# Sample attention in tiles of 128 cache positions with 4 KB rows, and conditioning slabs every two and a half chunks

## The chip, the cores and the metric

The kernel runs on one core of one Trainium2 chip. The metric is the device time of one execution, in microseconds; three runs of the kernel before gave 1655.76, 1656.50 and 1656.68 us, median 1656.5 us. Everything is float32.

## The reference

One layer of a hybrid decoder, for a prompt of 256 tokens and for 8 sample sequences of 4 new tokens each (32 rows), with the same weights. D_MODEL is 2048.

```python
mod = silu(c) @ w_ada + b_ada                      # 6 x 2048 columns: shift, scale, gate, twice
h = rmsnorm(x) * (1 + scale1) + shift1
qa, ka, va, qb, kb, vb, r, log_a = project(h)      # one matrix w_in, 2048 x 6160
oa = mix_a(qa, ka, va)                             # 16 heads of 64: attention, three dilations merged
ob, gla_state = mix_b(qb, kb, vb, log_a)           # 4 heads: gated linear attention
x = x + gate1 * merge_out(oa, ob, r)               # w_out, 2048 x 2048
h2 = rmsnorm(x) * (1 + scale2) + shift2
x = x + gate2 * conv_ffn(h2)                       # w_up, convolution, w_down
```

For the samples, mix_a attends from each new token to a cache of 1024 past keys and values per sequence (`cache_k_win`, `cache_v_win`, shape 8 x 1024 x 16 heads x 64) and to the 4 new ones. Of the older 512 cache positions only 4 in 16 are ever seen, so 128 + 512 = 640 cache positions (CK) per sequence are used, that is KT = 5 tiles of 128.

## The kernel before

**Order of the work.** TensorE runs one long sequence and the other engines feed it. It computes the first conditioning columns, then the input projection in 96 chunks (the loop `for j in range(LAST)`), with the rest of the conditioning, the GLA heads and the prompt's attention pairs put between the chunks at fixed chunk numbers; then the sample attention in four groups of two sequences (the stage that the change rewrites); then the output projection, the up-projection and the down-projection. A weight product is three matmuls (L921 to L923) on a high and a low part of each operand; the parts of a weight chunk are made by ScalarE (L1453, L1461, L1470) and VectorE (L1995 and others) from a slab in `ring`.

**Conditioning slabs.** The later conditioning, 48 slabs of 4 x 512 columns of `w_ada` (1 MB each, rows of 2 KB), comes in pairs. `LATE_AT` gives the chunk after which TensorE uses slab r (`late_ada`, L872): 22, 22, 25, 25, ... 91, 91. Slab r goes into ring slot 1 or 3, and there is one pair of slots: ScalarE's queue issues the load of slab r (`late_load`, L1513) only when TensorE has used slab r - 2. After each fourth slab `late_turn` transposes the result. In the same code `in_load` loads the slabs of w_in into slots 0 and 2 from SyncE's queue, and GpSimd's queue moves the GLA states. `head(h, r)` is step r of GLA head h at chunk 28 + 8h + r, `pair(p, r)` is step r of pair p at chunk 63 + 4p + r. A pair computes scores at step 2 (L1113); VectorE and ScalarE make probabilities of them; step 4 transposes these (L1121); step 5 is the product with the values (L1130).

**Sample attention.** A group has 16 key units n: unit (i, j) is all 640 positions of one head pair of one sequence. `key_turns` transposes its five tiles (L1168) into two PSUM banks, of which units with even n are copied to `kcT` by ScalarE (L1643, L1645) and those with odd n by VectorE (L2255, L2257); both also copy 32 new keys behind them (L1644, L2256). `kcT` has 8 buffers, PSUM space is two units. `scores` (L1183) is eight matmuls per j, in two halves of 336 positions, accumulated over j = 0 to 3 in banks 4 and 5. When the last is done, VectorE adds the bias and takes the maximum (`maxima`, L2267, L2270), ScalarE takes the exponential (L1649), VectorE normalizes (L2277), TensorE transposes the probabilities (L1200), ScalarE copies them (L1654 to L1656), TensorE multiplies them with the values (L1213, then the new values, L1220), ScalarE copies the result (L1661) and TensorE transposes it (L1226). TensorE's order in a group g is: units 4 to 7 of g; probabilities and values of g - 1; units 8 to 11; output of g - 1; units 12 to 15; last scores; units 0 to 3 of g + 1. VectorE copies units, then runs maxima(g) before it copies the first units of g + 1.

**Loads of the stage.** SyncE's queue issues them in its program's order. A slab u of keys is one sequence with half of the heads (512 columns, rows of 2 KB): 256 KB for the old positions and 1 MB for the near ones (L606, L607), in ring slot u. The values come likewise in pieces of 256 and 512 KB (L629, L630, L635) into `vals`, which lies over the space of hhi and hlo. The keys of g + 1 are issued as the units of g that use the slot are transposed, the values of g when `values` of g - 1 has passed tile 2 (`v0`) and its end (`v`). The first keys wait for the last two conditioning slabs (`raw_used`, slots 1 and 3) and for the last w_in slabs (slots 0 and 2); the first values wait for TensorE's last chunks. Before the values of the last group SyncE issues two slabs of `w_ada` (`gate_load(0)`, `gate_load(1)`), after them two of w_out (`out_half`) and two more of w_ada.

## Time and profile before

| | |
|---|---|
| median of three runs | 1656.5 us (1655.76 to 1656.68) |
| the profiled execution | 1655.58 us, span 1654.0 us |
| mean granted TensorE clock | 0.994 |
| TensorE (PE) busy | 1612.3 us (97%) |
| VectorE (DVE) busy | 891.0 us (54%) |
| ScalarE (ACT) busy | 719.2 us (43%) |
| DMA, mean over the span | 224 GB/s |
| issue to landing, ring<-in_w_ada from ACT's queue, 58 | median 8.4 us |
| issue to landing, ring<-in_cache_k_win, 1 MB, 16 | median 9.8 us |

PE is the matmuls, PEld the weight loads that overlap them, "q" behind an engine's name its DMA-issuing queue. A busy PE is not PE at its peak: matmul ends are modelled and overlap, so short idle times vanish in the busy share and are read from starts in the timeline instead. "PEclk" is the granted TensorE clock as a share of full speed, 1.00 being 2.4 GHz and 0.50 being 1.2 GHz. A load's time to landing runs from its issue to the arrival of its last part.

### The profile page before, as it was taken

To read this page: it belongs to the slowest core of one execution; us is meant where nothing else is said; L and a number is where in the kernel's file an instruction comes from. 1 tells how busy PE (TensorE), PEld (TensorE's weight loads), DVE (VectorE), ACT (ScalarE), POOL (GpSimd) and SP (SyncE) were. 2 spreads that over 40 slices of the span, in tenths; PEclk is the share of its full clock that TensorE was granted. 3 is DMA by queue.
4 is the path that set the end of the run, shared out by engine and by line. 5 is a ranking of instruction groups with operands and counts; after the bars stand their busy time and mean duration, and the time that the engine had idled before them with its cause. 6 is when DMAs were issued, how large, how long until landed. Compare 5 with 4: busy or idle time off the path is not lost.

```text
span 1654.0 us, 29469 instructions
## 1 busy us (share of the span) xinstructions
PE 1612.3 (97%) x12258; PEld 1445.7 (87%) x12258; DVE 891.0 (54%) x1562; ACT 719.2 (43%) x1026; POOL 75.2 (5%) x132
## 2 busy tenths in 40 slices
PE   8999999999999889999999999999999999999997
PEld 4778888888888544998999999999999999999997
DVE  3555555455665443644754555545555466656563
ACT  3332444445555433534533433334333345555452
POOL 2000000000111000000000000000000000000000
PEclk8999999999999999999999999999999999999999
DMA  9998777778877999675845445454454545545550
GB/s 342 372 379 314 260 248 240 274 266 288 280 251 273 339 380 351 220 241 171 288 148 177 162 155 180 150 182 158 154 181 157 177 132 178 187 159 173 174 171 34
DMA packets 276113, 370.71 MB, mean 224 GB/s; under 512 B 8273, under 2 KB 192947, under 8 KB 275977
## 3 DMA queue, kind: packets, MB, share of 16 engines
q1 hardware_dynamic: 232928, 279.88, 50.6%
q10 hardware_dynamic: 35970, 71.45, 12.1%
q0 software_dynamic: 7088, 17.54, 3.2%
q8 instruction: 97, 1.59, 0.4%
q14 instruction: 30, 0.25, 0.0%
HBM read 358.96 MB, written 9.88 MB: 223 GB/s over the span
## 4 chain that ended last, share of the span: by engine, by line
PE 84%; issue 5%; DVE 4%; DMA 3%; ACT 2%; SPq 1%; POOL 0%; ACTq 0%; DVEq 0%; POOLq 0%
PE ps L921 23%; PE ps L922 22%; PE ps L923 22%; PE ps L872 4%; PE ps L1168 2%; DMA ring<-in_w_in 1%; PE ps L1183 1%; SPq L525 1%; PE ps L1213 1%; DMA vals<-in_w_ada 1%; DMA proj<-in_w_ada 1%; PE ps L879 1%; DVE wlo L1995 1%; ACT whi L1470 0%; PE ps L1097 0%
## 5 line engine op out<-in xcount | busy, mean ns | idle before, releaser
L921 PE MATMUL ps<-hhi,whi 128*128 128x288 f32 x3136 | 934.7, 298 | 1.4 <-DVE hlo L1987 0.7
L922 PE MATMUL ps<-hlo,whi 128*128 128x288 f32 x3136 | 921.9, 294 | 0.0
L923 PE MATMUL ps<-hhi,wlo 128*128 128x288 f32 x3136 | 921.8, 294 | 0.0
L921 PEld LDWEIGHTS ps<-hhi,whi 128*128 128x128 f32 x3136 | 588.3, 188 | 40.0 <-issue 33.4
L922 PEld LDWEIGHTS ps<-hlo,whi 128*128 128x128 f32 x3136 | 588.5, 188 | 0.9
L923 PEld LDWEIGHTS ps<-hhi,wlo 128*128 128x128 f32 x3136 | 588.4, 188 | 0.0
L1856 DVE TENSOR_TENSOR wlo<-ring,whi 128x1024 fp32r<-128x1024 f32 x178 | 212.1, 1222 | 85.8 <-ACT whi L1453 85.4
L1453 ACT ACTIVATE whi<-ring 128x1024 fp32r<-128x1024 f32 x178 | 184.6, 1057 | 156.4 <-PE ps L923 156.4
L1995 DVE TENSOR_TENSOR wlo<-ring,whi 128x1024 fp32r<-128x1024 f32 x96 | 117.3, 1224 | 124.0 <-ACT whi L1470 123.9
L1470 ACT ACTIVATE whi<-ring 128x1024 fp32r<-128x1024 f32 x96 | 100.8, 1052 | 137.6 <-PE ps L923 112.7
L2484 DVE TENSOR_TENSOR wlo<-ring,whi 128x1024 fp32r<-128x1024 f32 (+1 forms) x94 | 105.7, 1131 | 56.0 <-ACT whi L1778 56.0
L1778 ACT ACTIVATE whi<-ring 128x1024 fp32r<-128x1024 f32 (+1 forms) x94 | 91.7, 980 | 73.8 <-PE ps L923 73.7
L2398 DVE TENSOR_TENSOR hlo<-proj,hhi 128x1152 fp32r<-128x1152 f32 (+3 forms) x56 | 60.9, 1100 | 47.5 <-ACT hhi L1725 46.6
L1725 ACT ACTIVATE hhi<-proj 128x1152 fp32r<-128x1152 f32 (+3 forms) x56 | 52.7, 954 | 49.7 <-PE ps L923 49.7
L2419 DVE TENSOR_SCALAR work<-work,small 128x304 f32<-128x304 f32 x44 | 17.3, 436 | 99.5 <-ACT work L1737 99.5
L872 PE MATMUL ps<-ring,c 128*32 128x512 f32 x544 | 68.7, 619 | 1.0 <-DMA ring<-in_w_ada 1.0
L1736 ACT ACTIVATE work<-ps 128x512 f32<-128x512 f32 x22 | 13.2, 599 | 109.3 <-PE ps L923 109.2
L2431 DVE TENSOR_TENSOR proj<-ps,work 128x512 f32<-128x512 f32 x22 | 15.2, 692 | 84.3 <-PE ps L923 84.3
L1168 PEld LDWEIGHTS ps<-con,ring 128*128 128x128 f32 x320 | 35.2, 143 | 24.1 <-issue 12.4
L1461 ACT ACTIVATE whi<-ring 128x1024 fp32r<-128x1024 f32 x32 | 33.2, 1055 | 47.9 <-PE ps L923 29.2
L1168 PE MATMUL ps<-con,ring 128*128 128x128 f32 x320 | 43.8, 283 | 8.5 <-DVE kcT L2257 5.8
L1863 DVE TENSOR_TENSOR wlo<-ring,whi 128x1024 fp32r<-128x1024 f32 x32 | 38.1, 1221 | 16.4 <-ACT whi L1461 16.3
(312 smaller groups left out, 1184.4 us busy)
## 6 DMA issues: line engine op xcount, KB each, us to landing
ring<-in_w_up SPq DMA_DIRECT2D x88, 1024.0 KB, 5.1
ring<-in_w_ada ACTq DMA_DIRECT2D x58, 1024.0 KB, 8.4
ring<-in_w_in SPq DMA_DIRECT2D x48, 1024.0 KB, 9.2
ring<-in_w_down SPq DMA_DIRECT2D x32, 1408.0 KB, 6.7
ring<-in_cache_k_win SPq DMA_DIRECT2D x16, 1024.0 KB, 9.8
vals<-in_cache_v_win SPq DMA_DIRECT2D x32, 512.0 KB, 8.3
ring<-in_w_out SPq DMA_DIRECT2D x16, 1024.0 KB, 6.0
proj<-in_w_ada SPq DMA_DIRECT2D x14, 1024.0 KB, 10.7
```

The source lines that it names most:

```text
L872: last = mm(ps[32 * k:32 * k + 32, bank, :], c32[:, 4 * (s % 4) + k, :], rows[:, k, :], start=(s % 4 == 0), stop=(s % 4 == 3))
L921: mm(out, w_hi, x_hi, start=start, stop=False)
L922: mm(out, w_hi, x_lo, start=False, stop=False)
L923: return mm(out, w_lo, x_hi, start=False, stop=stop)
L1168: last = turn(ps[:, 2 * (n % 2) + t // 4, P * (t % 4):P * (t % 4) + P], slab(u, KT, 512)[:, t, P * m:P * m + P], ident)
L1453: f(whi[:, j % BUFS, 0:n], ring[:, s % SLOTS, n * (j % 2):n * (j % 2) + n], ACT.Copy).then_inc(hi_done, 1)
L1470: f(whi[:, j % BUFS, :].rearrange("p (k c) -> p k c", k=4), in_chunk_of(rows, j), ACT.Copy).then_inc(hi_done, 1)
L1778: f(whi[:, jj % BUFS, 0:n], ring[:, s % SLOTS, CHUNK * kc:CHUNK * kc + n], ACT.Copy).then_inc(hi_done, 1)
L1856: v.tensor_tensor(wlo[:, j % BUFS, 0:n], ring[:, s % SLOTS, n * (j % 2):n * (j % 2) + n], whi[:, j % BUFS, 0:n].bitcast(F32), ALU.subtract ...
L1995: v.tensor_tensor(wlo[:, j % BUFS, :].rearrange("p (k c) -> p k c", k=4), in_chunk_of(rows, j), whi[:, j % BUFS, :].bitcast(F32).rearrange ...
L2398: last = v.tensor_tensor(hlo[:, at:at + m, :], actT[:, k0:k0 + m, :], hhi[:, at:at + m, :].bitcast(F32), ALU.subtract)
L2484: v.tensor_tensor(wlo[:, jj % BUFS, 0:n], ring[:, (2 * kg + h) % SLOTS, CHUNK * kc:CHUNK * kc + n], whi[:, jj % BUFS, 0:n].bitcast(F32), A ...
```

## The change

Keys, values and scores of a group are cut by tiles of 128 cache positions instead of by head halves. A slab `t` of keys or values holds 128 positions of both sequences of the group with all heads: 1 MB in rows of 4 KB (tile 0, the old positions, in two DMAs of 512 KB). A key unit is eight transposes into two PSUM banks, the first bank copied by ScalarE and the second by VectorE, each in one copy of 512 columns; there are 10 units in a group. Scores follow two units behind the transposes and run across the border between groups; the new keys are multiplied straight from `kS` (`new_scores`), not copied. `kcT` shrinks to four buffers. maxima, softmax and normalization of g - 1 are placed between the copies of group g, and two buffers `qd` take turns. SyncE's order of loads and their waits follow the tiles. And `LATE_AT` puts the pairs of conditioning slabs at chunks 22, 24, 27, 29, ... 79.

```diff
-        vals = sb("vals", [P, 4, KT * 512])
-        kcT = sb("kcT", [P, 8, CK + NS])
+        valsf = sb("vals", [P, 2 * KT * 1024])
+        kcT = sb("kcT", [P, 4, 1024])
...
-        qd = projf[:, kv0:kv0 + 512]
+        qd = [projf[:, kv0 + 512 * n:kv0 + 512 * n + 512] for n in range(2)]
...
-        LATE_AT = [22 + r // 2 * 3 for r in range(48)]
+        LATE_AT = [22 + r // 2 * 5 // 2 for r in range(48)]
...
-        def key_tile(n):
-            j, i = n // 4, n % 4
-            return i, j, 2 * (i // 2) + 1 - j // 2, 2 * (i % 2) + j % 2
+        def key_unit(n, e):
+            return [(2 * e + q // 2, n // 4 * 2 + q % 2, n % 4) if n < 8 else (q, KT - 1, 2 * (n - 8) + e) for q in range(4)]
...
-        HALF_KEYS = (CK + NS) // 2
+        KEY_AT = (1, 4, 0, 3, 2)
+        VALUES_AT = (0, 5120, 2048, 7168)
+        ringf = ring[:, :, :].rearrange("p s c -> p (s c)")
+        def key_slab(t):
+            return ringf[:, 2048 * KEY_AT[t]:2048 * KEY_AT[t] + 2048].rearrange("p (b c) -> p b c", b=2)
+        def value_slab(t):
+            if t < KT - 1:
+                return valsf[:, VALUES_AT[t]:VALUES_AT[t] + 2048].rearrange("p (b c) -> p b c", b=2)
+            return valsf.rearrange("p (b c) -> p b c", b=2)[:, :, 4096:5120]
+        def arrived(t, g):
+            return (g + 1) * (32 if t == 0 else 16)
...
-            def key_loads(g, us):
-                for u in us:
-                    sp.wait_ge(*ST.upto(f"k{8 * (1 - u % 2) + 5 + u // 2 * 2}", g - 1))
-                    key_load(g, u)
...
+            def cache_tile(cache, g, t, dst, landed):
+                if t == 0:
+                    for b in range(2):
+                        far = a[cache][0][2 * g + b, 0:PAST // 2].rearrange("(a r) h d -> a r (h d)", r=16)[:, 0:TS]
+                        sp.dma_start(dst[:, b, :], far).then_inc(landed, 16)
+                else:
+                    s_ = PAST // 2 + P * (t - 1)
+                    near = a[cache][0][2 * g:2 * g + 2, s_:s_ + P].rearrange("b p h d -> p b (h d)")
+                    sp.dma_start(dst, near).then_inc(landed, 16)
+            def keys(g, t):
+                cache_tile("cache_k_win", g, t, key_slab(t), keys_in[t])
+            def values(g, t):
+                cache_tile("cache_v_win", g, t, value_slab(t), vals_in[t])
+            sp.wait_ge(raw_used, RAW_OUT - 1)
+            keys(0, 0)
+            sp.wait_ge(raw_used, RAW_OUT)
+            keys(0, 1)
+            sp.wait_ge(lo_done, CH_OUT - 2)
+            keys(0, 2)
+            sp.wait_ge(lo_done, CH_OUT)
+            keys(0, 3)
+            keys(0, 4)
             sp.wait_ge(used, CH_OUT + BUFS - 2)
-            values_first(0, (0, 2))
+            values(0, 0)
+            values(0, 1)
             sp.wait_ge(used, CH_OUT + BUFS)
-            values_first(0, (1, 3))
-            values_last(0)
-            key_loads(1, (1, 3, 0, 2))
-            with sp.Fori(1, NB // 2 - 1) as g:
-                key_loads(g + 1, (1, 3))
-                value_loads(g)
-                key_loads(g + 1, (0, 2))
-            gate_load(0)
-            gate_load(1)
-            value_loads(NB // 2 - 1)
-            sp.wait_ge(*ST.upto("k15", 3))
+            for t in range(2, KT):
+                values(0, t)
+            for g in range(NB // 2):
+                more = g < NB // 2 - 1
+                if more:
+                    sp.wait_ge(*ST[1].upto("k3", g))
+                    keys(g + 1, 0)
+                    keys(g + 1, 1)
+                    sp.wait_ge(*ST[1].upto("k7", g))
+                    keys(g + 1, 2)
+                    keys(g + 1, 3)
+                else:
+                    gate_load(0)
+                    gate_load(1)
+                if g:
+                    sp.wait_ge(*SO.upto("v0", g - 1))
+                    for t in range(3):
+                        values(g, t)
+                    sp.wait_ge(*SO.upto("v", g - 1))
+                    for t in range(3, KT):
+                        values(g, t)
+                if more:
+                    sp.wait_ge(*ST[1].upto("k9", g))
+                    keys(g + 1, 4)
+            sp.wait_ge(*ST[1].upto("k7", 3))
             out_half(0)
+            sp.wait_ge(*ST[1].upto("k9", 3))
             out_half(1)
...
             def key_turns(g, n):
-                i, j, u, m = key_tile(n)
-                if j % 2 == 0 and i % 2 == 0:
-                    pe.wait_ge(far_in[u], g * 16 + 16)
-                    pe.wait_ge(full[u], g * 16 + (SL_SAMP // SLOTS * 16 + 16 - LESS[u]))
-                pe.wait_ge(*SK[n % 2].upto(f"k{(n - 2) % 16}", g if n >= 2 else g - 1))
-                for t in range(KT):
-                    last = turn(ps[:, 2 * (n % 2) + t // 4, P * (t % 4):P * (t % 4) + P],
-                                slab(u, KT, 512)[:, t, P * m:P * m + P], ident)
-                last.then_inc(*ST.step(f"k{n}"))
-            def scores(g, j, half):
-                if j + half == 0:
+                for t in {0: (0, 1), 4: (2, 3), 8: (4,)}.get(n, ()):
+                    pe.wait_ge(keys_in[t], arrived(t, g))
+                for e in range(2):
+                    pe.wait_ge(*SK[e].upto(f"k{(n - 2) % 10}", g if n >= 2 else g - 1))
+                    for q, (i, t, j) in enumerate(key_unit(n, e)):
+                        c = P * head_pair(i, j)
+                        last = turn(ps[:, 2 * (n % 2) + e, P * q:P * q + P], key_slab(t)[:, i // 2, c:c + P], ident)
+                    last.then_inc(*ST[e].step(f"k{n}"))
+            def query(g, i, j):
+                return qd[g % 2][:, 32 * (4 * i + j):32 * (4 * i + j) + 32]
+            def scores(g, n):
+                if n == 0:
                     pe.wait_ge(*SQ.upto("qd", g))
                     pe.wait_ge(*SV.upto("biased", g - 1))
-                if half == 0:
-                    for e in range(2):
-                        pe.wait_ge(*SK[e].upto(f"k{4 * j + 2 + e}", g))
-                cols = slice(HALF_KEYS * half, HALF_KEYS * half + HALF_KEYS)
-                for i in range(4):
-                    q = qd[:, 32 * (4 * i + j):32 * (4 * i + j) + 32]
-                    last = mm(ps[32 * i:32 * i + 32, 4 + half, 0:HALF_KEYS], q, kcT[:, (4 * j + i) % 8, cols],
-                              start=(j == 0), stop=(j == 3))
-                if half:
-                    last.then_inc(*ST.step(f"b{j}"))
-            def key_batch(g, j):
-                for half in range(2):
-                    for n in range(2):
-                        key_turns(g, 4 * j + 2 * half + n)
-                    if j:
-                        scores(g, j - 1, half)
+                for e in range(2):
+                    pe.wait_ge(*SK[e].upto(f"k{n}", g))
+                if n < 8:
+                    for i in range(4):
+                        last = mm(ps[32 * i:32 * i + 32, 4, 256 * (n // 4):256 * (n // 4) + 256], query(g, i, n % 4),
+                                  kcT[:, (2 * g + n) % 4, 256 * i:256 * i + 256], start=(n % 4 == 0), stop=(n % 4 == 3))
+                else:
+                    for j in (2 * (n - 8), 2 * (n - 8) + 1):
+                        for i in range(4):
+                            c = 512 * (j % 2) + P * i
+                            last = mm(ps[32 * i:32 * i + 32, 5, 0:P], query(g, i, j), kcT[:, (2 * g + n) % 4, c:c + P],
+                                      start=(j == 0), stop=(j == 3))
+                last.then_inc(*SB.step(f"s{n}"))
+            def new_scores(g):
+                for j in range(4):
+                    for i in range(4):
+                        mm(ps[32 * i:32 * i + 32, 5, P:P + NS], query(g, i, j), kS[:, head_pair(i, j), :],
+                           start=(j == 0), stop=(j == 3))
...
-                for u in range(4):
-                    pe.wait_ge(vals_in[u], g * 32 + 32)
                 for t in range(KT):
-                    if t == 3:
-                        pe.wait_ge(last_vals_in, g * 64 + 64)
+                    pe.wait_ge(vals_in[t], arrived(t, g))
                     for i in range(4):
-                        rows, b, at = slice(32 * i, 32 * i + 32), i // 2, 512 * t + 256 * (i % 2)
-                        last = mm(ps[rows, 7, :], sT[:, t, rows], vals[:, 2 * b:2 * b + 2, at:at + 256],
-                                  start=(t == 0), stop=False)
+                        rows, at = slice(32 * i, 32 * i + 32), 256 * (i % 2)
+                        v_rows = value_slab(t)[:, i // 2, :].rearrange("p (h c) -> p h c", h=2)[:, :, at:at + 256]
+                        last = mm(ps[rows, 7, :], sT[:, t, rows], v_rows, start=(t == 0), stop=False)
...
-            key_batch(0, 0)
             for g in range(NB // 2):
-                key_batch(g, 1)
-                if g:
-                    probabilities(g - 1)
-                    values(g - 1)
-                key_batch(g, 2)
-                if g:
-                    output(g - 1)
-                key_batch(g, 3)
-                for half in range(2):
-                    scores(g, 3, half)
-                if g < NB // 2 - 1:
-                    key_batch(g + 1, 0)
+                for n in range(0, 10, 2):
+                    key_turns(g, n)
+                    key_turns(g, n + 1)
+                    if n or g:
+                        for m in range(2):
+                            scores(g if n else g - 1, (n - 2) % 10 + m)
+                    if n == 2:
+                        new_scores(g)
+                    if n == 4 and g:
+                        probabilities(g - 1)
+                    if n == 6 and g:
+                        values(g - 1)
+                    if n == 8 and g:
+                        output(g - 1)
+            for m in range(2):
+                scores(NB // 2 - 1, 8 + m)
...
             def key_copy(g, n):
-                i, j = key_tile(n)[0:2]
-                act.wait_ge(*ST.upto(f"k{n}", g))
-                act.wait_ge(*ST.upto(f"b{(j - 2) % 4}", g if j >= 2 else g - 1))
-                f(kcT[:, n % 8, 0:512], ps[:, 0, :], ACT.Copy)
-                f(kcT[:, n % 8, CK:CK + NS], kS[:, head_pair(i, j), :], ACT.Copy)
-                f(kcT[:, n % 8, 512:CK], ps[:, 1, 0:P], ACT.Copy).then_inc(SK[0].sem, 1)
+                act.wait_ge(*ST[0].upto(f"k{n}", g))
+                act.wait_ge(*SB.upto(f"s{(n - 4) % 10}", g if n >= 4 else g - 1))
+                f(kcT[:, (2 * g + n) % 4, 0:512], ps[:, 2 * (n % 2), :], ACT.Copy).then_inc(*SK[0].step(f"k{n}"))
...
-            key_copy(0, 0)
-            key_copy(0, 2)
             for g in range(NB // 2):
-                key_copy(g, 4)
-                key_copy(g, 6)
+                for n in range(4):
+                    key_copy(g, n)
+                if g:
+                    softmax(g - 1)
+                for n in range(4, 6):
+                    key_copy(g, n)
                 if g:
                     probabilities(g - 1)
+                for n in range(6, 8):
+                    key_copy(g, n)
+                if g:
                     output(g - 1)
-                for n in range(8, 16, 2):
+                for n in range(8, 10):
                     key_copy(g, n)
-                if g < NB // 2 - 1:
-                    key_copy(g + 1, 0)
-                softmax(g)
-                if g < NB // 2 - 1:
-                    key_copy(g + 1, 2)
+            softmax(NB // 2 - 1)
...
             def queries(g):
-                dve.wait_ge(*ST.upto("b3", g - 1))
+                if g >= 2:
+                    dve.wait_ge(*SB.upto("s9", g - 2))
...
             def key_copy(g, n):
-                i, j = key_tile(n)[0:2]
-                dve.wait_ge(*ST.upto(f"k{n}", g))
-                dve.wait_ge(*ST.upto(f"b{(j - 2) % 4}", g if j >= 2 else g - 1))
-                v.tensor_copy(kcT[:, n % 8, 0:512], ps[:, 2, :])
-                v.tensor_copy(kcT[:, n % 8, CK:CK + NS], kS[:, head_pair(i, j), :])
-                v.tensor_copy(kcT[:, n % 8, 512:CK], ps[:, 3, 0:P]).then_inc(SK[1].sem, 1)
+                dve.wait_ge(*ST[1].upto(f"k{n}", g))
+                dve.wait_ge(*SB.upto(f"s{(n - 4) % 10}", g if n >= 4 else g - 1))
+                v.tensor_copy(kcT[:, (2 * g + n) % 4, 512:1024], ps[:, 2 * (n % 2) + 1, :]).then_inc(*SK[1].step(f"k{n}"))
...
             queries(0)
-            key_copy(0, 1)
-            key_copy(0, 3)
             for g in range(NB // 2):
-                for n in range(5, 16, 2):
-                    if g and n == 13:
-                        output(g - 1)
+                for n in range(2):
                     key_copy(g, n)
-                maxima(g)
+                if g:
+                    maxima(g - 1)
+                for n in range(2, 4):
+                    key_copy(g, n)
+                if g:
+                    norm_scores(g - 1)
+                for n in range(4, 8):
+                    key_copy(g, n)
                 if g < NB // 2 - 1:
                     queries(g + 1)
-                    key_copy(g + 1, 1)
-                norm_scores(g)
-                if g < NB // 2 - 1:
-                    key_copy(g + 1, 3)
+                for n in range(8, 10):
+                    key_copy(g, n)
+                if g:
+                    output(g - 1)
+            maxima(NB // 2 - 1)
+            norm_scores(NB // 2 - 1)
             output(NB // 2 - 1)
```

## Rows read from the trace of the kernel before

**Rows 1.** Windows: us; PE, PEld, DVE, ACT, POOL busy; PEclk, DMA share, GB/s.
```profile
156.00:546.00 390.00, 384.44 (x2978) 320.27 (x2976) 217.41 (x482) 197.78 (x331) 38.41 (x58) 1.00 0.78 268
...
564.10:590.50 26.40, 22.80 (x207) 12.40 (x203) 11.98 (x46) 10.68 (x31) 0.00 (x0) 1.00 0.89 313
590.50:616.80 26.30, 22.49 (x205) 12.37 (x202) 11.93 (x46) 9.40 (x30) 0.00 (x0) 1.00 1.05 399
616.80:643.00 26.20, 22.89 (x194) 12.76 (x193) 11.93 (x46) 9.40 (x30) 0.00 (x0) 0.93 1.02 373
```
**Rows 2.** Timeline of PE, a group's inside and its border (start, us, what).
```profile
552.60 1.31 PE L1168 MATMUL ps<-con,ring 128*128 128x128 f32 x10
553.84 0.77 PE L1183 MATMUL ps<-kcT,proj 128*32 128x336 f32 x8
554.54 1.31 PE L1168 MATMUL ps<-con,ring 128*128 128x128 f32 x10
...
562.85 1.34 PE L1183 MATMUL ps<-kcT,proj 128*32 128x336 f32 x16 [0.46 <-DVE kcT L2257]
564.11 1.31 PE L1168 MATMUL ps<-con,ring 128*128 128x128 f32 x10
...
568.01 1.64 PE L1168 MATMUL ps<-con,ring 128*128 128x128 f32 x10 [1.33 <-DVE kcT L2257]
...
570.54 0.77 PE L1183 MATMUL ps<-kcT,proj 128*32 128x336 f32 x8
...
575.05 4.50 PE L1213 MATMUL ps<-vals,work 128*32 128x512 f32 x40 [0.99 <-ACT work L1656]
...
580.47 0.33 PE L1168 MATMUL ps<-con,ring 128*128 128x128 f32 x1
```
**Rows 3.** Groups by form, 564 to 616.8 us: the two copies (busy, mean ns).
```profile
L2255 DVE COPY kcT<-ps 128x512 f32<-128x512 f32 x16 | 11.1, 692 | 24.7 <-PE ps L1168 24.7
L1643 ACT ACTIVATE kcT<-ps 128x512 f32<-128x512 f32 x16 | 9.5, 594 | 18.7 <-PE ps L1168 18.6
```
**Rows 4.** DMA view: the first line 547.08 to 548.5 us, the second 639.74 to 639.80.
```profile
vals<-in_cache_v_win SPq DMA_DIRECT2D x1, 512.0 KB, 11.1
...
vals<-in_cache_v_win SPq DMA_DIRECT2D x1, 512.0 KB, 9.7
```
**Rows 5.** Timeline of PE: the stage's last transposes.
```profile
656.14 0.65 PE L1226 MATMUL ps<-con,proj 128*128 128x128 f32 x4
```
**Rows 6.** Windows, columns as in rows 1: a stall and the clock after it.
```profile
617.00:621.00 4.00, 2.15 (x17) 1.71 (x17) 3.87 (x17) 2.60 (x8) 0.00 (x0) 1.00 1.05 407
621.40:624.80 3.40, 3.39 (x19) 1.88 (x17) 1.84 (x6) 0.88 (x3) 0.00 (x0) 0.50 1.05 408
```
**Rows 7.** Timeline: conditioning pairs on PE, and the issue of a second slab.
```profile
372.44 1.92 PE L872 MATMUL ps<-ring,c 128*32 128x512 f32 x16
385.83 1.92 PE L872 MATMUL ps<-ring,c 128*32 128x512 f32 x16
...
446.05 1.92 PE L872 MATMUL ps<-ring,c 128*32 128x512 f32 x16
...
448.04 0.38 ACTq L1513 DMA_DIRECT2D ring<-in_w_ada  x1
```
**Rows 8.** DMA view, second slabs issued at 448.04 and 287.18 us: time to landing.
```profile
ring<-in_w_ada ACTq DMA_DIRECT2D x1, 1024.0 KB, 8.7
...
ring<-in_w_ada ACTq DMA_DIRECT2D x1, 1024.0 KB, 13.9
```
**Rows 9.** Timeline of PE: scores and probability transposes of pairs 4 and 7.
```profile
472.77 0.93 PE L1113 MATMUL ps<-proj 64*128 64x128 f32 x8
...
482.11 0.82 PE L1121 MATMUL ps<-con,proj 128*128 128x128 f32 x6
...
535.62 0.93 PE L1113 MATMUL ps<-proj 64*128 64x128 f32 x8
542.91 0.82 PE L1121 MATMUL ps<-con,proj 128*128 128x128 f32 x6
```

64 lines of the change are left out of this document (13 added, 51 removed).

## The prediction

> **What bounds the kernel now.** The windows by stage come first. In the input projection PE is busy 384.4 of 390 us and the DMA engines have room, at 0.78. In the sample stage that turns round: a group takes 26.4, 26.3 and 26.2 us, PE's busy time leaves over 3 us of each open, and the DMA share is 1.05 and 1.02 in the last two, at 399 and 373 GB/s [rows 1]. So two things set this stage: TensorE's order with its stops, and the loads. The timeline shows the stops, which the busy share hides. Inside a group, ten transposes and a half of scores repeat every 1.94 us [rows 2]. At the border they don't: the last scores begin at 562.85, and six units' transposes, 30 x 0.107 = 3.2 us of work, fill the 6.3 us from 564.11 to 570.4, just before the next scores, waiting for VectorE's copies, which stand behind maxima. Together with the 0.46 us before the last scores that is 3.5 us a group. The probabilities' copy costs another 1 us before 575.05, as nothing is put between.
>
> **The new order on TensorE.** A group has 80 transposes before and after (16 x 5, now 10 x 8) and 8 x 336 = 2688 columns of scores, each four matmuls side by side (now 8 x 256 + 4 x 128 + 4 x 32 = 2688). By the rows a transpose is 0.107 us (a period of 1.94 less 0.70 of scores and 0.17 of changing over, by ten) and 336 columns of scores 0.56 us plus 0.14 of changing over. After: five rounds of 16 x 0.107 + 0.17 + 0.85 + 0.14 = 2.87 us, 14.4 us in all, where eight rounds of 1.94 made 15.5. No row shows matmuls of 32 columns in groups of four; from their columns the 16 of new_scores are 0.2 us, as the same columns cost them before, and at most 0.9 us, one change-over each; I take 0.5, nearer the rate of the 336-column rows. Values and their new rows stay at 5.4 us (575.05 to 580.47 [rows 2]), probabilities 0.6, output 0.45. A group is then 21.4 us on TensorE if nothing waits. The waits: a copy is 0.59 us on ScalarE and 0.69 on VectorE [rows 3], two of each a round of 2.87 us, so the two PSUM pairs are free in time. maxima now stands behind two copies; its 1.9 us of bias and maximum lie beside two units of transposes, 1.7 us, and two scores, 0.85 us. The probabilities' copy has a whole round before values. With these hidden, PE's own chain through four groups would be 20 us shorter than now. If the cover of VectorE is gone, a round waits about 0.7 us, one copy.
>
> **The loads don't follow.** A group needs 5 MB of keys and 5 of values, 10.5 million bytes. In 21.4 us that would be 490 GB/s; the highest figure in my rows is 408 and a whole group reached 399 [rows 1, 6]. So the loads take the place of PE's waits. What must land between the last values of the first group and those of the last is 15 + 15 + 2 slabs of 1 MB (the two gate slabs are issued ahead of the last values), 33.6 million bytes. Before, it ran from 558.2 (547.1 + 11.1) to 649.4 (639.8 + 9.7) [rows 4], 91.2 us, a mean of 368 GB/s, with an idle time of 2 to 3 us before the second key slabs of group 2, since these waited for transposes. After, the first group's values land some 4 us earlier, at 554, because its keys no longer crowd them: with conditioning over at chunk 79, two key slabs are issued at 506, when SyncE is through with the slabs of w_in, instead of 523. And the keys of g + 1 are asked for from unit 3 on, so the queue doesn't run dry. At 399 GB/s, 84 us from 554 ends at 638; at 373 it is 90 us and 644. No row has loads with 4 KB rows; below, I allow them 373, the slowest of the busy groups, above, the 408 of rows 6. I take 393, near the busiest group, and 640.5. Behind the last tile stand one value product, the new values, a copy and the last transposes, 3 us, so the stage ends near 643.5 instead of 656.6 [rows 5]: 13 us less, 9.5 to 16 with the ends of the rate. The Trainium skill (DMA: Bandwidth & Descriptors, section Bandwidth) gives about 358 GB/s as HBM's limit for one core; by that the loads would end at 648 and 5 to 6 us would be gained. The trace disagrees, with 399 GB/s over 26 us [rows 1].
>
> **The clock.** Before, PE stopped for half of a stretch of 4 us, and the granted clock was then 0.50 of full speed, 1.2 GHz, for 3.4 us [rows 6]; that is at most 1.7 us of work lost. After, PE waits about 5 us for the last values, and the same can follow. I charge 1.5 us (0 to 4). The Trainium skill (TensorE: Matmul & The Clock Gate, section HAM oscillation — how this bites in real kernels) says that a wait for DMA takes the clock down, so that the work behind it runs cold; by that a load-bound end is dearer than PE's idle time alone. The rows show one such fall, behind a wait for copies.
>
> **The conditioning slabs.** This is the part that can lose. The work of 48 slabs and 12 late_turns stays, so their moving costs nothing itself; ScalarE's 46 DMA issues move with them, and its queue waits no longer than now, as each waits for a slab that TensorE has just used. But a pair's successor is asked for only when it is used, and the gaps are now alternately two and three chunks. The second slab is issued 2.0 us after the pair's start [rows 7] and takes 8.7 us in a plain case, 13.9 in the worst [rows 8], where states are moved too. It is needed 0.9 us after the next pair's start. So a gap must be 9.8 us in the plain case. The shortest three-chunk gaps are 13.4 us (372.44 to 385.83 [rows 7]); without one bare chunk of 24 matmuls at 0.131, 3.2 us with its change, a gap is 10. From the chunks' own times I get 9.2 (chunk 27 to 29), 9.6 (37), 9.2 (62), 10.3 (52), 10.1 (77) and 10.8 or more for the other seven of the twelve. In the plain case 27, 37 and 62 lose 0.2 to 0.6 each; 37 and 52 lie beside state moves and lose up to 2 and 3 us. Below, nothing is lost; above 6.5 us; I take 2.5, of which 0.5 is no loss, since TensorE waits for VectorE in chunk 54 anyway. Second, in chunks 82 to 91 slabs cover a wait of the pairs. In pair 4 the step from scores to probability transposes took 9.3 us with slabs between; in pair 7, with none, it took 7.3 [rows 9], hardly more than the 6.5 of two bare chunks, so VectorE's chain can be just in time; where it first splits a weight chunk, 1.2 us on the page (L1856), it is that much late. Three pairs lose their cover: 0 to 1.2 us each, and I take 0.5. That makes 3.5 us, 0 to 10.
>
> **Moved and free.** Out_half(0) is asked for earlier, and it lands after the last values as before, some 3 us ahead of its use; gate slabs 2 and 3 land four slabs behind the last values, near 651, and are used behind the first product of the output stage, when before they landed no earlier against the stage's end. SyncE's issues fall from 20 to 12 a group, and wait beside everything. The GpSimd queue is moved past nothing. The 32-column copies go, on engines that wait for PE anyway.
>
> **The sum.** Against the profiled execution's own 1655.6 us: -13 in the stage, +1.5 clock, +3.5 chunks, that is -8. One more us for two effects that I could not place, the slabs' packet unevenness and a tile landing later than its neighbours on some engines: -7. The profiled execution lies 0.9 us under the median of 1656.5, so the forecast is **1649.5 us**.
>
> **Rivals.** (1) Loads no faster: 4 KB rows run at 373 and the clock falls twice. Stage -9.5, clock +3, chunks +3.5: -3, about 1653.5, or near no change with the chunks at 6. For it: groups with the same packets differed by 7% [rows 1]. Against: 368 included the idle time. 0.14. (2) Slower, by one mechanism: the second conditioning slab comes late in every short gap. It decides from 12 us to landing in the plain case. The densest traffic is now 3.25 MB in two and a half chunks instead of 3.5 in three. At 12.5 us each of ten gaps loses 2.5 to 3.5 us, 30 in all; less the 13 of the stage, +17. At 11.5 it is 18 and the result is about +4, 1660. For it: 13.9 has been seen [rows 8]. Against: that was beside a state read, the plain one is 8.7, and the median of all 58 such loads in the small table is 8.4. 0.09. (3) The loads hardly matter and TensorE's chain counts: it would need 490 GB/s for all of its 20 us, but at 408 with no stalls of slabs and no clock loss it comes to -16, 1640. 0.09. The likeliest case keeps 0.68, with 1643 to 1653. That the change doesn't do what it says is excluded by the code: the waits and the order are written out by hand.
>
> **The numbers.** A measurement of this kernel can tell 0.2%, 3.3 us. Faster: the likeliest case, all but its upper edge, and rival 3: 0.78. Same: 0.13. Slower: 0.09. The range 1641 to 1657 takes in the likeliest case, most of rivals 1 and 3, and leaves out about 0.2.
>
> **What would show it.** Right: groups of 22 to 27 us whose length follows the landing of keys and values, DMA share over 1 from 555 to 640, no wait of L1168 for VectorE at a border, a stop before the last values' products, the last L1226-like transposes near 645 plus what the chunks lose. The conditioning slabs' waits for DMA are at chunks 39 and 54, if anywhere. Wrong: waits for DMA at most of the short gaps; copies that hold up transposes; groups at 21.4 us; or a product stage that begins where it did, as out_half or the squares become the last to arrive.

## The result, and the profile after

The changed kernel takes 1660.9 us against 1656.0 for the kernel before: the ratio is 1.0039 (95% interval 1.0028 to 1.0049), slower by 0.4%. I had forecast 1649.5 and a range of 1641 to 1657. The sample attention did what I had expected. The conditioning slabs cost over four times what I had put down for them.

The profiled execution of the changed kernel took 1660.2 us with a span of 1658.6, so 4.6 us more of span than before. To see where they are, I cut both spans at the same places: the first product of weight chunk 22, of chunk 62, of chunk 95, the first transposes of cached keys, and the first product of head_sums (L1261 before, L1269 after). The first fence has the windows of the kernel before between these cuts, the second those of the changed kernel. The granted clock of a window is its share of full speed. The columns are us; PE, PEld, DVE, ACT, POOL busy with counts; granted clock, DMA share, GB/s.

```profile
152.90:374.30 221.40, 218.09 (x1723) 181.19 (x1721) 118.97 (x248) 105.21 (x179) 13.96 (x20) 1.00 0.76 259
374.30:539.70 165.40, 164.54 (x1246) 137.90 (x1243) 99.61 (x236) 90.93 (x148) 25.58 (x40) 1.00 0.82 275
546.20:660.20 114.00, 100.03 (x850) 55.54 (x850) 51.12 (x187) 43.10 (x125) 0.51 (x1) 0.99 0.99 361
```

```profile
152.90:387.50 234.60, 226.36 (x1770) 185.00 (x1769) 118.97 (x249) 105.07 (x180) 13.94 (x20) 0.99 0.78 265
387.50:555.60 168.10, 159.49 (x1197) 134.76 (x1196) 100.31 (x234) 91.62 (x148) 25.66 (x40) 1.00 0.73 246
562.00:665.00 103.00, 97.31 (x1106) 63.35 (x1107) 48.41 (x132) 39.63 (x70) 1.01 (x2) 0.97 1.01 392
```

Read down the lengths. The sample stage is 11.0 us shorter (114.0 to 103.0), what lies behind it is unchanged (993.8 and 993.6), and the 15.9 us lost lie ahead of it: 13.2 between chunks 22 and 62 (221.4 to 234.6), 2.7 between chunks 62 and 95 (165.4 to 168.1). Both reach chunk 22 at 152.9 us. The granted clock is lower on the way there in the changed kernel, 0.93 against 0.97, and no time is lost by it; the DMA share is 1.00 in both.

Now the busy time, which separates two kinds of loss. Between 22 and 62 two pairs of slabs and two late_turns more are run than before (16 pairs for 14), at 1.95 and 0.81 us each 5.5 us of moved work; the other 7.7 us are waits and a slower clock. Between 62 and 95 it turns round: PE has 5.0 us less to do (164.5 to 159.5) and still takes 2.7 longer. Before, PE stood idle there for 0.9 us, now for 8.6. **The slabs that were moved out of the late chunks had cost next to nothing there, and they cost their full price where they went.** The 15.9 us are then 7.7 of waits and clock up to chunk 62, and 8.2 (5.5 and 2.7) for work that was moved out of its cover.

The waits of PE in the chunk phase of the changed kernel (us in total, times, longest) name both. Before, no slab waited for DMA there, and L1107 (now L1113) and L1121 (now L1127) waited for nothing.

```profile
PE ps L878 <- DMA ring<-in_w_ada: 6.7, 4, 3.5
PE ps L1103 <- DVE proj L2166: 2.8, 3, 0.9
PE ps L1113 <- DVE proj L2173: 2.7, 2, 1.3
PE ps L1045 <- DVE proj L2148: 1.5, 2, 1.2
PE ps L1136 <- DVE proj L2169: 1.4, 1, 1.4
PE ps L1127 <- DVE proj L2210: 1.4, 3, 0.9
```

The longest wait for a slab, at chunk 39, in PE's timeline, then the second slab's entry in the DMA view (KB, us from issue to landing; issued at 241.5), then the windows behind it.

```profile
249.60 1.06 PE L878 MATMUL ps<-ring,c 128*32 128x512 f32 x8
254.14 1.21 PE L878 MATMUL ps<-ring,c 128*32 128x512 f32 x8 [3.47 <-DMA ring<-in_w_ada]
```

```profile
ring<-in_w_ada ACTq DMA_DIRECT2D x1, 1024.0 KB, 12.6
```

```profile
253.00:255.00 2.00, 0.86 (x8) 0.16 (x8) 0.23 (x1) 0.00 (x0) 0.00 (x0) 0.98 1.07 371
255.00:257.00 2.00, 2.00 (x11) 1.73 (x8) 0.23 (x2) 1.14 (x4) 0.00 (x0) 0.50 1.06 376
257.00:259.00 2.00, 2.00 (x13) 2.00 (x11) 0.71 (x3) 0.46 (x2) 0.00 (x0) 0.66 1.10 351
```

The gap from chunk 37 to 39 is short, two reads of states and two slabs of w_in share the DMA engines with the pair (share 1.07 as the wait ends), and the second slab takes 12.6 us where the plain case of before took 8.7 [rows 8]. PE then runs at half of full speed, 1.2 GHz, for 3.4 us, which is at most 1.7 us of work lost. The other waits of this kind are 0.9 us in chunk 29 and 2.4 in chunk 54.

The lost cover, in the timeline of the late chunks: pair 4's scores (L1119), its probabilities' transposes (L1127), the next pair's first sums (L1103).

```profile
489.72 0.93 PE L1119 MATMUL ps<-proj 64*128 64x128 f32 x8
498.03 0.87 PE L1127 MATMUL ps<-con,proj 128*128 128x128 f32 x6 [0.87 <-DVE proj L2210]
499.83 1.24 PE L1103 MATMUL ps<-proj,con 128*128 128x288 f32 x4 [0.93 <-DVE proj L2166]
```

Before, the same step took 9.3 us with slabs between and without a wait [rows 9]. Now it takes 8.3, one of them waiting.

The stage itself. Two windows of one group's length after the first: PE has no idle time in them, and 21.2 us take the place of 26.3 [rows 1].

```profile
586.00:607.20 21.20, 21.20 (x274) 14.15 (x266) 11.35 (x34) 8.08 (x16) 0.00 (x0) 1.00 0.99 385
607.20:628.50 21.30, 21.30 (x274) 14.15 (x266) 10.88 (x33) 8.09 (x16) 0.00 (x0) 1.00 1.03 415
```

And its end: the last values' products, the idle products behind, the first head_sums.

```profile
651.15 1.06 PE L1219 MATMUL ps<-vals,work 128*32 128x512 f32 x8 [0.56 <-DMA vals<-in_cache_v_win]
653.62 1.06 PE L1219 MATMUL ps<-vals,work 128*32 128x512 f32 x8 [1.40 <-DMA vals<-in_cache_v_win]
656.16 1.07 PE L1219 MATMUL ps<-vals,work 128*32 128x512 f32 x8 [1.48 <-DMA vals<-in_cache_v_win]
...
660.41 4.79 PE L866 MATMUL ps<-con 128*128 128x256 f32 x12
665.04 2.10 PE L1269 MATMUL ps<-proj,con 128*128 128x288 f32 x8
```

Three tiles are waited for, 3.4 us in all, and the products on them start 2.5 us apart, as the loads come at 1 MB in 2.5 us. Behind them twelve idle-product records take 4.79 us where they took 2.76 before: the clock is at half there, from 657.7 on for 6.8 us.

### The profile page after: what moved, and what is told of

Same layout as the page of the kernel before. It is cut to its first block, busy times and chain, and to the rows that moved or that the text cites. A ratio compares the mean times of both kernels' runs of the same rounds, so it can differ in the third digit from the quotient of the medians.

```text
span 1658.6 us, 29769 instructions
## 1 busy us (share of the span) xinstructions
PE 1615.9 (97%) x12514; PEld 1456.2 (88%) x12514; DVE 887.9 (54%) x1506; ACT 714.4 (43%) x970; POOL 75.2 (5%) x132
## 4 chain that ended last, share of the span: by engine, by line
PE 83%; DMA 5%; issue 5%; DVE 3%; ACT 2%; SPq 1%; POOL 0%; ACTq 0%; DVEq 0%; POOLq 0%
PE ps L927 23%; PE ps L929 22%; PE ps L928 22%; PE ps L878 5%; DMA vals<-in_cache_v_win 2%; DMA ring<-in_w_ada 2%; PE ps L1173 1%; DMA vals<-in_w_ada 1%; PE ps L885 1%; PE ps L1188 1%; DVE wlo L2001 1%; SPq L537 1%; PE ps L1219 1%; PE ps L872 0%; PE ps L866 0%
## 5 line engine op out<-in xcount | busy, mean ns | idle before, releaser
L1742 ACT ACTIVATE work<-ps 128x512 f32<-128x512 f32 x22 | 13.2, 598 | 109.3 <-PE ps L929 109.2
L2261 DVE COPY kcT<-ps 128x512 f32<-128x512 f32 x40 | 27.2, 689 | 33.9 <-PE ps L1173 33.5
L2430 DVE SCALAR_TENSOR_TENSOR work<-work,small 128x304 f32<-128x304 f32 x88 | 43.2, 532 | 1.6
## 6 DMA issues: line engine op xcount, KB each, us to landing
vals<-in_cache_v_win SPq DMA_DIRECT2D x16, 1024.0 KB, 12.5
proj<-in_w_ada SPq DMA_DIRECT2D x14, 1024.0 KB, 11.5
```

## The experiments

My theory from the comparison: the new sample attention gains 11 us, and the new places of the slabs lose 16 in two ways that add up, slabs that land late in short gaps (with the clock behind the longest wait) and cover taken from the head pairs' chain. The rivals are written into the expectations. The table sums up; the stretches are those of the profiled execution of each kernel, cut as above, and the ratios are to the kernel before, with 95% intervals.

| run | what it is | ratio | 22 to 62 | 62 to 95 | stage |
|---|---|---|---|---|---|
| before | | 1 | 221.4 | 165.4 | 114.0 |
| changed | | 1.0039 (1.0028–1.0049) | 234.6 | 168.1 | 103.0 |
| third_chunk | slabs back at every third | 0.9927 (0.9914–0.9941) | 222.5 | 165.5 | 103.0 |
| slabs_alone | old attention, new slabs | 1.0131 (1.0111–1.0152) | 235.3 | 170.6 | 116.0 |
| cover_back | last four pairs back | 0.9994 (0.9985–1.0003) | 234.3 | 165.6 | 101.0 |
| free_filler | products added, large | 1.0062 (1.0042–1.0082) | 234.4 | 175.9 | 104.5 |
| filler_as_slabs | products added, as slabs | 1.0035 (1.0022–1.0048) | 234.5 | 170.4 | 103.5 |
| light_slabs | half the slabs' bytes | 0.9955 (0.9938–0.9972) | 226.2 | 168.4 | 103.6 |
| one_pair_later | pair 39 to 40 | 1.0020 (1.0008–1.0032) | 231.5 | 170.1 | 102.3 |
| half_rows | third_chunk, 2 KB rows | 0.9956 (0.9941–0.9971) | 222.0 | 165.5 | 104.4 |
| gates_early | third_chunk, gate slabs earlier | 0.9915 (0.9900–0.9929) | 222.3 | 165.5 | 98.7 |
| cover_heads | third_chunk, 14 pairs earlier | 0.9922 (0.9908–0.9935) | 219.5* | 164.8 | 102.0 |
| gates_and_heads | both | 0.9901 (0.9883–0.9919) | 225.8* | 164.8 | 98.6 |

*These two run one pair of slabs less between the cuts and one late_turn more, since the pair of chunk 22 is at chunk 21.

### The two halves of the change apart

```diff
-        LATE_AT = [22 + r // 2 * 5 // 2 for r in range(48)]
+        LATE_AT = [22 + r // 2 * 3 for r in range(48)]
```

> The changed kernel with the conditioning slabs back at every third chunk, so the new sample attention alone. My theory: the changed kernel lost 15.8 us between chunks 22 and 95 and gained 11.0 us from there to the first head_sums; with the old slab schedule the 15.8 come back, and only the first two key slabs have less lead (asked for at 523, 23 us before the stage in place of 38). So 1660.9 - 15.8 = 1645.1, plus 0 to 3: 1643 to 1648, ratio to the kernel before 0.993. Rival one, the early end of conditioning is what feeds the new sample attention (keys from 506, as I had argued): then the stage is longer than 103 us by several, 1650 to 1654. Rival two, the chunk phase is slow because of something else in the change (the layout of the ring or of projf): the stage still starts near 560 and the time is near 1661.

It took 1643.75 us, ratio 0.9927, in the range that I had given: the new attention alone makes the kernel faster by 0.7%. The windows between the cuts are those of before up to the stage and those of the changed kernel in it.

```profile
374.40:539.90 165.50, 164.64 (x1247) 138.00 (x1244) 99.61 (x236) 91.00 (x148) 25.66 (x40) 1.00 0.81 277
546.30:649.30 103.00, 97.28 (x1107) 62.73 (x1108) 47.40 (x131) 38.64 (x69) 0.51 (x1) 0.97 1.01 392
```

So both rivals fall: an early end of conditioning isn't needed to feed the new stage (103.0 us with keys asked for 23 us ahead of it, 103.0 with 38), and nothing else in the change slows the chunks.

The reverse, the slabs of the changed kernel in the kernel before:

```diff
-        LATE_AT = [22 + r // 2 * 3 for r in range(48)]
+        LATE_AT = [22 + r // 2 * 5 // 2 for r in range(48)]
```

> The kernel before with its own sample attention and the slabs of the changed kernel, every two and a half chunks. My theory: the losses of the chunk phase do not depend on the sample attention, so the stage starts some 15.8 us later, at 562, and then takes its 110 us or up to 1 us less, since the keys have longer: 1670 to 1672, ratio 1.009. Rival (the loads of the old stage gain from the early end, since they mattered more than its waits for copies): 1662 to 1667.

It took 1678.25 us, ratio 1.0131, over the upper end of what I expected. The chunk phase lost 19.1 us (13.9 and 5.2) in place of 15.9, so the loss doesn't need the new attention, and it is not the same in every execution. The stage lost another 2.0: at three group borders, behind waits for VectorE's copies, the granted clock falls to 0.50 for 3.4 us, where the kernel before had one such fall [rows 6]. Two of its windows at a border:

```profile
585.00:588.00 3.00, 1.67 (x11) 1.09 (x10) 2.68 (x13) 2.56 (x6) 0.00 (x0) 0.88 0.88 326
588.00:591.00 3.00, 3.00 (x19) 1.69 (x17) 1.58 (x6) 0.88 (x3) 0.00 (x0) 0.56 0.06 25
```

By the ratios the halves together (0.9927 and 1.0131) make 1.0058, the changed kernel is at 1.0039. That difference of 3 us is little more than the intervals allow. In the traces 2.0 us of the kind are in the stage, whose falls at group borders the new attention's order doesn't have, and 3.2 in the chunk phase, where their cause stays open.

### The cover

```diff
-        LATE_AT = [22 + r // 2 * 5 // 2 for r in range(48)]
+        LATE_AT = [22 + r // 2 * 5 // 2 if r < 40 else 22 + r // 2 * 3 for r in range(48)]
```

> The changed kernel with the first 20 pairs of slabs two and a half chunks apart (chunks 22 to 69) and the last four at chunks 82, 85, 88 and 91, as before. My theory (two losses that add up): the late second slabs of chunks 29, 39, 54, 64 and 69 and the clock behind them stay, some 7.5 us in all; the 8.3 us of lost cover are back. So 1660.9 - 8.3 = 1652.6, 1650 to 1655. Rival (late slabs are nearly all of the loss, the rest follows from them): 1658 to 1662. Rival (the cover is nearly all of it): 1645 to 1648.

It took 1655.3 us, ratio 0.9994. The time lies between those of the two rivals, so both fall, but it came 2.7 us over my figure, just past the end of its range. Against the changed kernel it is 5.6 us by the medians and 7.5 by the ratios, and its profiled span is 5.2 us shorter. Only 2.5 of these lie between chunks 62 and 95; 2.0 are in the stage, where the clock fell for 3.4 us and not for 6.8. The cuts say more. Up to chunk 62 nothing changes (234.3). From 62 to 95 the same eight pairs are run as in the changed kernel, four of them later, in 165.6 us and not 168.1. That is as long as the kernel before takes with ten pairs. The cover that came back at chunks 82 to 91 was partly taken from 72 to 79: the waits from chunk 62 on are now

```profile
PE ps L1103 <- DVE proj L2166: 2.0, 3, 0.9
PE ps L878 <- DMA ring<-in_w_ada: 1.3, 1, 1.3
PE ps L1127 <- DVE proj L2210: 0.9, 1, 0.9
```

From chunk 83 to 87, with no slabs, the changed kernel takes 20.8 us, of which PE is busy for 17.7; the kernel before, with slabs, takes 20.1 and is busy for all of them. The first window is before, the second changed.

```profile
478.84:498.96 20.12, 20.12 (x157) 17.08 (x153) 12.97 (x30) 13.05 (x22) 3.21 (x5) 1.00 0.82 284
```

```profile
493.84:514.64 20.80, 17.68 (x130) 15.73 (x129) 13.55 (x34) 12.54 (x20) 3.91 (x7) 1.00 0.45 137
```

A head pair's chain through VectorE and ScalarE takes some 20 us with these slabs or without, and a pair of slabs less shortens nothing. Neither engine is busy all the time (13.6 and 12.5 us in the second window), so I read it as the steps' following one another, not as an engine's throughput.

Then the direct test, work added where the changed kernel has lost its slabs.

```diff
+                if j in (82, 85, 88, 91):
+                    pe.wait_ge(*BV.upto(*late("mod", 11)))
+                    idle_products(3, 8)
```

> The changed kernel with eight idle products of 256 columns added after each of chunks 82, 85, 88 and 91, where the kernel before has its last four pairs of slabs: 4 x 2.0 = 8 us of extra TensorE work, nothing else. My theory (VectorE's and ScalarE's chain of a head pair sets some 20 us per four chunks there, and TensorE has slack): the extra work is free, 1661 to 1662, no wait of L1103, L1113 or L1127 is left in chunks 83 to 91. Rival (the waits there are a fixed delay that each pair adds whatever TensorE does, or come from the earlier loads of w_in and the keys): the products cost their full price, 1668 to 1669.

It took 1668.75 us, just what the rival had said (three of the four executions lie at 1668.7 to 1669.0, one at 1662.67; with that one the ratio is 1.0062). But the size of the filler was wrong: PE's busy time from 62 to 95 is up by 12.3 us (159.5 to 171.8) and the stretch by 7.8 (168.1 to 175.9). So I repeated it with products of the right size:

```diff
+                if j in (82, 85, 88, 91):
+                    pe.wait_ge(*BV.upto(*late("mod", 11)))
+                    for n in range(8):
+                        mm(ps[32 * (n % 4):32 * (n % 4) + 32, 3, :], c32[:, n, :], con[:, 0:512], start=True, stop=True)
```

> The first filler was larger than I had said (a product of 256 columns is two records of 0.2 us or more, so a chunk got 3.4 us and not 2.0); it left room for both readings. Here the changed kernel gets, behind chunks 82, 85, 88 and 91, the very products of a pair of slabs: eight of 128 x 512, 1.95 us by the trace of before, but with rows that are already in SBUF, so no load. My theory (the pair's chain is the bound there): of 7.8 us at most 1.1 show, since the kernel before passes from chunk 82 to 95 in 66.1 us with the slabs and the changed one in 65.0 without; 1661 to 1663. Rival (full price): 1668.7. What would stand between, 1664 to 1666: half of the work is covered.

1662.8 us, ratio 1.0035 against the changed kernel's 1.0039: four times eight products of 128 x 512 don't show in the ratio, and the median is in the range of my theory. In its trace, the window from chunk 62 to 95, and the waits of the pairs' lines of over half a microsecond from chunk 79 to 95:

```profile
386.00:556.40 170.40, 166.56 (x1261) 136.36 (x1260) 100.38 (x234) 91.56 (x148) 25.65 (x40) 1.00 0.72 242
```

```profile
PE ps L1136 <- DVE proj L2173: 1.5, 1, 1.5
PE ps L1103 <- DVE proj L2170: 0.9, 1, 0.9
```

PE does 7.1 us more (166.6) in 2.3 us more, and of these 1.5 are later slabs at chunks 69 and 79, ahead of the first filler. The waits of L1113 and L1127 are gone, and of L1103's 2.8 us 0.9 are left; L1136's 1.4 us stay, at chunk 92, behind the last filler. This is the cover, shown. The larger filler gives its size: of 12.3 us, 7.8 show, 2.2 of these again at chunks 69 and 79 (8.2 and 7.7 us for 7.0 and 6.6), so 6.7 were free.

### The late slabs

In light_slabs each of the 46 slabs that ScalarE asks for carries half its bytes; the conditioning values of these columns are then not those of the reference.

```diff
-                act.dma_start(slab(slot, 4, 512), w_ada[:, 4 * (r % 4):4 * (r % 4) + 4, at:at + 512]
+                act.dma_start(slab(slot, 4, 512)[:, 0:2, :], w_ada[:, 4 * (r % 4):4 * (r % 4) + 2, at:at + 512]
```

> The changed kernel, with each of the 46 slabs that ScalarE asks for carrying only two of its four 128-row parts (half the bytes; the conditioning output is left wrong in these columns). TensorE's work and the order of all issues stay. My theory: the waits of the slabs' products for DMA (6.7 us) and the clock at 0.50 behind the longest one are the stalls of chunks 29, 39, 40 and 54; with half the bytes the second slab lands in 6 to 7 us and they are gone, so 7 to 8 us less than 1660.9: 1653 to 1654. The uncovered waits of chunks 83 to 92 stay. Rival (the wait comes from when the slabs are asked for and from the other loads in the queues, not from their size): 1657 to 1660.

1650.6 us, ratio 0.9955, 0.84% or 14 us under the changed kernel by the ratios and 10 by the medians, more than the 7 to 8 that I expected. In the trace 22 to 62 is 8.4 us shorter (226.2):

```profile
152.90:379.10 226.20, 224.39 (x1771) 183.85 (x1770) 118.61 (x249) 105.07 (x180) 13.93 (x20) 1.00 0.63 207
```

So late slabs and the clock behind them cost 8.4 us there. What is left is 4.8 us over the 221.4 of the kernel before. That is most of the 5.5 us of work moved in, although slabs now cover the 2.1 us for which L1089 and L1046 waited before: here the moved work is paid nearly in full. The waits of the slabs are gone but for 0.3 us, and the waits of the pairs have stayed:

```profile
PE ps L1103 <- DVE proj L2166: 2.8, 3, 0.9
PE ps L1127 <- DVE proj L2210: 2.3, 3, 1.2
PE ps L1045 <- DVE proj L2148: 1.5, 2, 1.2
...
PE ps L878 <- DMA ring<-in_w_ada: 0.3, 1, 0.3
```

So the bytes in flight make the lateness. The trace shown has only 7.4 us less span than that of the changed kernel. It is the longest of four executions (1647.8 to 1652.7), and in it the clock fell for 3.4 us at 490.7, behind two of pair 4's waits, 0.9 us each; a lost cover can take the clock with it too.

```diff
-        LATE_AT = [22 + r // 2 * 5 // 2 for r in range(48)]
+        LATE_AT = [22 + r // 2 * 5 // 2 + (r // 2 == 7) for r in range(48)]
```

> The changed kernel with one pair of slabs moved: the one of chunk 39 to chunk 40, so its gap is 19 us long in place of 9. In the trace of the changed kernel this pair waits 3.5 us for DMA, with 0.4 us of other waits, and the granted clock is 0.50 for 3.4 us right behind it (1.7 us lost). Theory (the clock falls because of that wait): both go, 5.5 us, and the next pair, of chunk 42, is asked for later but has 14 us: 1655 to 1656. Rival (the clock falls in some stretch of the heads anyway): 1657. If the wait moves to the pair of chunk 42 instead: 1658 or more.

1660.1 us, ratio 1.0020, 0.2% and not 0.3 under the changed kernel: a miss. It is in the range that I had given for a wait that moves to chunk 42, but no such wait is there (the chunk takes 8.9 us in both). The wait of 3.5 us is gone (chunk 39 takes 3.3 us, not 9.0, of which 1.95 are the moved slabs). But chunk 41 takes 9.7 and not 7.2, and the clock falls all the same, seven microseconds later. In all, 22 to 62 is 3.1 us shorter, and 62 to 95 is 2.0 longer, with another fall of 3.4 us at 497.4, behind pair 4's waits. The timeline at the first fall and its windows:

```profile
261.63 0.39 PE L1018 MATMUL ps<-proj 128*128 128x32 f32 x2
261.86 1.15 PE L1065 MATMUL ps<-proj 128*128 128x256 f32 x2
```

```profile
260.00:262.00 2.00, 2.00 (x18) 1.84 (x18) 1.49 (x3) 0.44 (x1) 0.00 (x0) 0.98 1.02 390
262.00:264.00 2.00, 2.00 (x9) 1.17 (x12) 1.87 (x5) 0.10 (x1) 0.00 (x0) 0.50 0.58 144
```

PE waits for nothing before this fall. What it does from 259.1 on are late_turn's products of 9 columns and a head's products of 32 columns. So the second rival is right that the clock can fall in a head's stretch anyway; that it fell behind the wait in the changed kernel is seen, that it wouldn't have fallen there without it isn't shown.

### The sample stage

```diff
-                    sp.dma_start(dst, near).then_inc(landed, 16)
+                    for c in (0, 512):
+                        sp.dma_start(dst[:, :, c:c + 512], near[:, :, c:c + 512]).then_inc(landed, 16)
...
-            return (g + 1) * (32 if t == 0 else 16)
+            return (g + 1) * (64 if t == 0 else 32)
```

> The version with slabs at every third chunk (third_chunk, ratio 0.9927), with each tile of keys and of values loaded in two DMAs of 512 columns, so rows of 2 KB as in the kernel before, the same bytes in the same order, and 24 issues a group in place of 12. If the row size matters: the kernel before moved 373 to 399 GB/s in its busy groups, 4 KB rows 411 to 415, so the 45 us from 595 to the last values take 2 to 5 us longer, and the extra issues take 7 us of SyncE a group beside everything; 1646 to 1650. If it does not: within 1 us of third_chunk.

1649.8 us, ratio 0.9956 against 0.9927, in the range for a row that matters. The two loads of tile 0, not shown, are halved in the same way. The first fence has its windows, the second those of third_chunk:

```profile
595.00:617.00 22.00, 20.91 (x266) 14.01 (x262) 10.31 (x28) 8.08 (x16) 0.00 (x0) 1.00 1.05 398
617.00:640.00 23.00, 20.34 (x172) 10.22 (x166) 4.82 (x16) 3.64 (x8) 0.00 (x0) 0.85 1.05 402
```

```profile
595.00:617.00 22.00, 22.00 (x278) 14.41 (x274) 10.38 (x28) 8.08 (x16) 0.00 (x0) 1.00 1.03 416
617.00:640.00 23.00, 18.64 (x174) 8.02 (x166) 4.82 (x16) 3.64 (x8) 0.00 (x0) 1.00 1.03 410
```

Rows of 2 KB move 398 and 402 GB/s at a share of 1.05, rows of 4 KB 416 and 410 at 1.03. The last values' last product starts at 643.45, not 640.43. Shorter rows in twice as many DMAs lower the rate by 2 to 4%; the edit halves both the row and the DMA, so which of the two does it isn't shown. This profiled execution was the fastest of its four, so how much of the 0.3% is the edit's own I leave at 1.4 us (the stage, 104.4 for 103.0) to 5.

Then a version that should beat both: the two gate slabs, which go ahead of the last values, are asked for in the first group's key loads, where the queue has gaps.

```diff
                     keys(g + 1, 1)
+                    if g == 0:
+                        gate_load(0)
...
                     keys(g + 1, 3)
-                else:
-                    gate_load(0)
-                    gate_load(1)
+                    if g == 0:
+                        sp.wait_ge(k_out, 256)
+                        gate_load(1)
```

> The version with slabs at every third chunk (1643.75), and gate slabs 0 and 1 asked for in the first group's key loads (one behind keys(1, 1), one behind keys(1, 3)) in place of ahead of the last group's values. Reading of its trace: from 595 to 640 the loads run without a gap at 2.5 us per 1 MB, and the last four tiles of values are waited for; between 554 and 577 the queue has gaps of some 7 us. Theory: the two slabs fill those gaps, the last values land 5 us earlier, the waits of 3.4 us ahead of the last products and the clock at 0.50 behind them go: 1636 to 1639. Rival (the bytes are only pushed on, values of group 1 come late in their place): 1642 to 1644.

1641.8 us, ratio 0.9915, just under the rival's range and over my theory's. In its trace the loads run without a gap from 555 on, and the last values are there in time: one run of 40 records without a wait, and no 0.50 of the clock in the stage.

```profile
575.00:595.00 20.00, 20.00 (x260) 13.24 (x249) 9.83 (x31) 7.02 (x15) 0.00 (x0) 1.00 1.03 415
617.00:638.00 21.00, 18.99 (x191) 9.14 (x194) 5.51 (x17) 3.92 (x9) 0.00 (x0) 1.00 1.03 412
```

```profile
635.53 4.50 PE L1221 MATMUL ps<-vals,work 128*32 128x512 f32 x40
...
645.83 1.45 PE L1271 MATMUL ps<-proj,con 128*128 128x288 f32 x5 [0.85 <-ACT proj L1695]
```

The stage is 98.7 us, 4.3 less than third_chunk's. The comparison gives 0.12%, 2 us, of that; the intervals overlap, so the gain is seen in the trace and not shown by the times. Theory and rival each had a part: the waits ahead of the last products are gone, and one tile of the third group's values is waited for 1.3 us instead.

```diff
-        LATE_AT = [22 + r // 2 * 3 for r in range(48)]
+        LATE_AT = [(21 if r < 28 else 22) + r // 2 * 3 for r in range(48)]
```

> The version with slabs at every third chunk, but the first 14 pairs one chunk earlier (21, 24, ... 60) and the other ten as before (64, 67, ... 91). In the trace of before TensorE waits for VectorE 1.0 us in chunk 36, 0.9 in 48, 1.6 in 54 and 1.0 in 60, all of them now chunks with a pair of slabs. If slabs cover a wait wherever it stands in the chunk phase: 3 to 4.5 us less than 1643.75, 1639 to 1641. Rival (the products of the slabs stand ahead of the head's steps in the chunk, so they delay VectorE's input as much as they give it time, or the waits move to the chunks that lost theirs): 1643 to 1646.

1643.5 us, ratio 0.9922 against 0.9927: no difference that can be told, and the rival's range. In the profiled execution the stretch from 22 to 62 fell from 222.5 to 219.5, and the waits of 36 and 48 are gone. But 1.1 us of that is work that the earlier places put outside the cuts (a pair out, a late_turn in), which leaves 1.9; the median moved by 0.3 us, and what executions differ by (1641.6 to 1647.7) is more than what can be had there.

> Both changes of the last call on third_chunk: gate slabs 0 and 1 in the first group's key loads, and the first 14 pairs of slabs one chunk earlier. Alone they gave 2.0 us and 0.8 us less than third_chunk (ratios 0.9915 and 0.9922 against 0.9927). They lie in different stretches and should add: 1640 to 1642, ratio 0.991. If the gate slabs only help where the stage begins as late as in that run: 1642 to 1643.

1640.8 us, ratio 0.9901 (0.9883 to 0.9919), the fastest of all: 1.0% under the kernel before. It can't be told from gates_early. Its profiled execution was a long one; in it the clock was at half for 3.4 us from 305.8 on, and for 6.8 us from 353.6 on, in chunk 57, which took 13.4 us where cover_heads took 9.2.

## Why the prediction was wrong

**The new order on TensorE: right.** I had a group at 21.4 us if nothing waits; from one group's values (589.77) to the next (610.94) it is 21.2. The waits for VectorE's copies at the borders are gone, new_scores took 0.4 us (0.5 expected), and a round 2.9.

**The loads: right at the end, wrong in the middle.** I let them set the pace from the second group on, at 393 GB/s. They moved 385 and 415 in the two groups' windows shown above, and PE waited for no load in either: groups at 21.4 us were on my list of signs that I was wrong, and these two took 21.2 and 21.3. The first waits for loads, 0.7 us, come behind 628.5, and in earnest, 3.4 us, only at the last three tiles. The stretch that I had added up came out close: the first group's values are in at 572.2 (asked for at 559.86, 12.4 us), the last at 656.1 (639.11 and 17.0), so 33.6 million bytes took 83.9 us, 400 GB/s. In third_chunk, which starts the stage where the kernel before does, it was 554.8 to 640.4, and I had written 554 to 640.5. Some of that fit is luck: 393 GB/s makes 85.5 us and 639.5 and not 640.5, and by the same sum the upper end, 408, gives 17 us and not 16. The stage with its clock was to give 11.5 us (13 less 1.5), and gave 11.0. For the rate I had also weighed the Trainium skill (DMA: Bandwidth & Descriptors, section Bandwidth) with its 358 GB/s. The same section says that a core alone, with the other core of its pair idle, reached 425 GB/s on 16 MB; that is the sentence which this kernel agrees with, at 410 to 416 in third_chunk and gates_early from 595 on.

**The clock: right in place, too small in size.** It fell to 0.50 for 6.8 us behind the waits for the last values; I had charged 1.5 us with 4 as the end, and the idle and real products behind took 3.4 us more. That it would fall in the chunk phase too (1.7 us at most) I hadn't counted.

**The conditioning slabs: this step failed.** I took 3.5 us, with 10 as the upper end, and it was 15.9. Without that term my sum gives 1646.0, and third_chunk, which doesn't move the slabs, took 1643.75. Both parts of the term were too small.

The first, late slabs: I took 2.5 us (up to 6.5). The waits for DMA are 6.7, with the clock behind them 8.4 (light_slabs); 7.7 of it show, as the moved slabs cover other waits. I had named the places: pairs 27, 37 and 52 begin the gaps whose ends stall, at 29, 39 and 54. The size was off since I set the plain 8.7 us to landing against each gap, and did not carry the 13.9 through where a state moves: by my own sum it needs a gap of 15.0, so the 9.6 and 10.3 after 37 and 52 would have lost 5, not "up to 2 and 3". In the gap after 37 came two reads of states and two slabs of w_in; it took 12.6 us and cost 3.5. This is the mechanism of my second rival, whose price began at 12 us. It struck three of the twelve short gaps hard, not ten.

The second, the cover, is the larger error (1.5 us taken, 8.2 measured), and it was one of thinking. I had asked what a few waits of a pair would be once its slabs are gone (3 x 0.5 us, from one pair's 7.3 us against 6.5 of two bare chunks). I should have asked what the moved work had cost where it stood. "The work of 48 slabs and 12 late_turns stays, so their moving costs nothing itself" was the false step. Four pairs and two late_turns left chunks 82 to 92, 9.4 us of work, and that stretch got shorter by 1.1 us (66.1 to 65.0 from chunk 82 to chunk 95). The same work was paid in full before chunk 62, where PE had been busy for 218.1 of 221.4 us. The pair that I took the 7.3 us from was the last one. No pair follows it, so VectorE has less to do beside it (4.6 us busy in the step): for pair 4 without cover the step is 8.3 us, with VectorE busy for 5.7, and waits.

**The rivals.** Rival 2 had the right side and the right place, but only half of the mechanism. Late slabs alone, 8.4 us, would not have eaten the stage's 11: light_slabs, which has next to none, is faster than before by 0.45%, and still slower than third_chunk by 0.28%. Rival 3 (TensorE's chain counts, the loads hardly) is true for the middle groups and not for the end: with the slabs left where they were, the kernel takes 1643.75 us, at the lower end of the likeliest case and 3.8 over that rival's 1640.

**What would show it.** I had listed waits for DMA at chunks 39 and 54, if anywhere; there they were, with 0.9 us at 29 beside them. I had not listed a wait of the pairs' lines for VectorE, which would have shown the other half.

## What to carry to other kernels

Before moving work, price it twice: what it costs where it goes, and what it costs where it stands. Work that stands beside another engine's chain is nearly free there, and taking it away gives nothing; the sign is a stretch in which the engine is busy all the time and yet waits as soon as something is taken out. And a load whose successor is asked for only at use has the whole gap as its budget: compare the shortest gap with the worst landing in that gap's own traffic, not with the median.

## What the hardware showed

- The granted clock fell to 0.50 with no wait of TensorE in the six microseconds before it: in one_pair_later PE was busy for all of 256 to 262 us, the last 2.7 with products of 9 and 32 columns, and stood at 0.50 in the window of 262 to 264. In gates_and_heads it fell at 305.8 in the same way, PE busy for all of the 6 us before, with the same two kinds of products at the end. In third_chunk the same step of the head as in one_pair_later, four microseconds earlier, had 1.00 in every window; what decides isn't known. The Trainium skill (TensorE: Matmul & The Clock Gate, section HAM oscillation — how this bites in real kernels) tells of falls behind a wait for DMA. The changed kernel agrees at 254.14 (3.47 us of waiting, then 0.50); the other two aren't of that kind.
- The same instructions can meet the clock differently when they are only shifted in time: the old attention had one fall in the profiled execution of the kernel before, and three in that of slabs_alone, where it began 19 us later.
- Loads of 1 MB in rows of 4 KB moved 416 and 410 GB/s, the same bytes in 512 KB loads with rows of 2 KB 398 and 402, in one order and at one place.
